# Router table by products, early expert weights, step sizes inside a branch, halves in a scan product, and merge joined with the last projection

## The reference

```python
# first block
h = rmsnorm(x, norm_mix_g) * (1 + sc1) + sh1
y = conformer_conv(h, ...)     # h @ w_in, gated; 31-tap causal conv per channel + b_dw;
                               # silu(layernorm(y)); @ w_out
x = x + g1 * y
h = rmsnorm(x, norm_ffn_g) * (1 + sc2) + sh2
x = x + g2 * hier_moe(h, ...)  # 4 groups x 8 experts, top 2 of the best group, hidden 512
x = rmsnorm(x, final_g)
# second block
h = rms_norm(x) * (1 + scale) + shift
q, k, v, z_att, q_idx, k_idx, w_idx, z_ssm, xbc, dt_raw, gate_logits = split(h @ w_in)
o_att = sparse_attention(...) * silu(z_att)    # an indexer keeps 256 keys for each query
y_att = o_att @ w_branch_att
dt = softplus(dt_raw + dt_bias);  a = -exp(a_log)
y = ssd(xs, dt, a, bm, cm)     # state-space scan, 32 heads of 64, chunks of 128 tokens
y_ssm = rms_norm((y + d_skip * xs) * silu(z_ssm)) @ w_branch_ssm
merged = sigmoid(g_att) * y_att + sigmoid(g_ssm) * y_ssm
x = x + gate * (merged @ w_out)
```

## Time and profile before

| | |
|---|---|
| median of 3 runs | 3097.91 us (3094.88 to 3101.71) |
| profiled execution | 3103.54 us, span 3101.7 us |
| granted TensorE clock, mean | 0.92 |
| TensorE busy | 2635.5 us, 85% of the span |
| VectorE | 1666.2 us, 54% |
| ScalarE | 898.8 us, 29% |
| POOL | 560.5 us, 18% |
| transfers | 430.96 MB, mean 139 GB/s |

### The profile page before, as it was taken

The page is one execution under the profiler, slowest core; times in us unless marked ns, Lnnn a source line. Parts: engine busy times, 40 slices in busy tenths (PEclk is TensorE's granted clock), DMA queues, the critical chain, the costliest instruction groups (busy, mean ns, idle before and its releaser), DMA issues. The chain is left out here.

```text
span 3101.7 us, 39507 instructions
## 1 busy us (share of the span) xinstructions
PE 2635.5 (85%) x15399; PEld 1471.3 (47%) x15399; DVE 1666.2 (54%) x2973; ACT 898.8 (29%) x1333; POOL 560.5 (18%) x504
## 2 busy tenths in 40 slices
PE   5996795598799995887999599969899899899869
PEld 3554344354455552443344377435545545545434
DVE  5884774122222325784999865234734744744651
ACT  5110402121112223333532255123423423423320
POOL 1111032200000002443421000002303303303202
PEclk8998796799999997898899799989999999999989
DMA  8562758399999995110022001320010010010051
GB/s 219 190 203 93 277 190 309 97 375 379 376 381 365 376 328 217 63 47 28 28 75 95 21 1 46 111 75 35 1 61 35 1 61 35 1 62 27 1 217 55
DMA packets 184152, 430.96 MB, mean 139 GB/s; under 512 B 27004, under 2 KB 35452, under 8 KB 183868
## 3 DMA queue, kind: packets, MB, share of 16 engines
q1 hardware_dynamic: 156972, 362.80, 32.7%
q0 software_dynamic: 11088, 33.84, 3.5%
q10 hardware_dynamic: 15936, 32.13, 3.0%
HBM read 370.82 MB, written 57.91 MB: 138 GB/s over the span
## 5 line engine op out<-in xcount | busy, mean ns | idle before, releaser
L1192 PE MATMUL m_gu<-arena,m_xT 128*64 128x256 f32 x1024 | 233.2, 387 | 20.4 <-DMA arena<-in_moe_w_up 18.0
L1194 PE MATMUL m_gu<-arena,m_xT 128*64 128x256 f32 x1024 | 233.2, 387 | 0.0
L2456 POOL TENSOR_TENSOR y_A<-adt,consts 128x1024 f32<-128x1024 f32 x32 | 64.5, 2014 | 882.1 <-POOLq L2240 731.1
L1270 DVE TENSOR_TENSOR m_hid<-m_sg,m_gu 64x256 f32<-64x256 f32 x96 | 39.6, 413 | 337.9 <-ACT m_sg L1240 337.9
L1194 PEld LDWEIGHTS m_gu<-arena,m_xT 128*64 128x64 f32 x1024 | 142.9, 140 | 73.8 <-issue 15.4
L1214 PE MATMUL m_y_ps<-arena,m_hidT 128*64 128x512 f32 x768 | 175.4, 598 | 0.0
L1925 DVE TENSOR_SCALAR_CACHE_REDUCE arena<-arena,s_cand 128x384 bf16<-128x384 f32 (+5 forms) x186 | 166.1, 943 | 2.2
L140 PE MATMUL i_pj<-hT,i_ws 128*128 128x512 f16 x384 | 148.3, 386 | 20.9 <-DVE i_ws L406 12.9
L1192 PEld LDWEIGHTS m_gu<-arena,m_xT 128*64 128x64 f32 x1024 | 142.9, 140 | 38.4 <-issue 27.5
L1240 ACT ACT_TABLE_LOAD x48 | 61.6, 1283 | 322.3 <-issue 274.0
L141 PE MATMUL i_pj<-hT,i_ws 128*128 128x512 f16 x384 | 148.8, 388 | 0.0
(11 more groups left out here) (491 smaller groups left out, 6540.7 us busy)
## 6 DMA issues: line engine op xcount, KB each, us to landing
arena<-in_moe_w_down SPq DMA_DIRECT2D x32, 2048.0 KB, 22.6
arena<-in_moe_w_gate SPq DMA_DIRECT2D x22, 2048.0 KB, 20.4
arena<-in_moe_w_up SPq DMA_DIRECT2D x22, 2048.0 KB, 24.5
hT<-in_moe_w_gate SPq DMA_DIRECT2D x10, 2048.0 KB, 20.1
hT<-in_moe_w_up SPq DMA_DIRECT2D x10, 2048.0 KB, 24.8
conv_y<-in_ada_w SPq DMA_DIRECT2D x8, 2048.0 KB, 7.9
x_tok<-in_ada_w ACTq DMA_DIRECT2D x6, 2048.0 KB, 12.6
slot_out<-m_y ACTq DMA_DIRECT2D x96, 128.0 KB, 6.2
```

Of the source, the lines that this page charges most:

```text
L1192: g = nc.tensor.matmul(gu_ps[i][g_rows, 0:FFN // 2], lhsT=xT[:, c, :], rhs=k.wg[e % WEIGHT_SLOTS][:, c, cols], start=c == 0, stop=c == KC - 1)
L1194: u = nc.tensor.matmul(gu_ps[i][u_rows, 0:FFN // 2], lhsT=xT[:, c, :], rhs=k.wu[e % WEIGHT_SLOTS][:, c, cols], start=c == 0, stop=c == KC - 1)
L2456: nc.gpsimd.tensor_tensor(A[:, s], per_head(k.adt, t, P), k.const("after").unsqueeze(1).to_broadcast([P, HPG, P]), ALU.mult) \
```

## The change

**Convolution and its norm.** The PSUM of the means (`k.mean_ps`) exists from the convolution on and doubles as an accumulator of the first tiles. The mean products of channel tiles 0 to 5 stand ahead of the last tile's taps and those of tile 6 behind them; the norm is left with tile 7's two. The last tile's y is evacuated in two halves and carried by SP and ScalarE (`last_half`) and not by POOL.

```diff
+            pe.wait_ge(u_done, last)
+            means(range(last - 1))
+            taps(last)
+            means(range(last - 1, last))
...
+            last_half(sp, 0)
+            sp.wait_ge(last_in[0], 16 * CG // 2)
...
+            last_half(act, 1)
+            act.wait_ge(last_in[1], 16 * CG // 2)
```

```diff
         def _(sp):
+            load_up(k, sp, 0)
+            load_down(k, sp, 0)
             for t in range(TT):
                 sp.wait_ge(normed_ready, t + 1)
-                sp.dma_start(normed_dram[t * P:(t + 1) * P, :], normed[:, t, :]).then_inc(stored, 16)
+                sp.dma_start(normed_dram[t * P:(t + 1) * P, :], normed[:, t, :]).then_inc(k.normed_stored, 16)
+            load_up(k, sp, 1)
+            load_down(k, sp, 1)
+            load_down(k, sp, 2)
             sp.dma_start(k.x_tok[:, :, :], natural).then_inc(k.x_natural, 16)
-            sp.wait_ge(stored, 16 * TT)
```

```diff
+            nc.tensor.matmul(pos_ps[:, :, :], lhsT=before16[:, :], rhs=mask[:, :, :], start=True, stop=False)
             for t in range(TT):
...
+                last = nc.tensor.matmul(pos_ps[:, t + 1:, :], lhsT=ones16[:, :],
+                                        rhs=mask[:, t:t + 1, :].to_broadcast([P, TT - t, EXPERTS]),
+                                        start=False, stop=t == TT - 1)
...
+            pe.wait_ge(hot, 1)
+            for n in range(2):
+                for t in range(TT):
+                    last = nc.tensor.matmul(tab_ps[:, :], lhsT=low_hot[:, n, t, :], rhs=blk_hot[:, n, t, :],
+                                            start=n == t == 0, stop=n == 1 and t == TT - 1)
...
+            step(v.tensor_tensor(low_hot[:, :, :, :].rearrange(flat), of_all(low, BLOCK), numbers(BLOCK), ALU.is_equal))
+            for n in range(2):
+                step(v.tensor_tensor(low_hot[:, n], low_hot[:, n], bc(tokid[:, :], BLOCK), ALU.mult))
+            v.tensor_tensor(blk_hot[:, :, :, :].rearrange(flat), of_all(blk, TABLE_ROWS), numbers(TABLE_ROWS),
+                            ALU.is_equal).then_inc(hot, 1)
```

```diff
                 last.then_inc(done, 1)
+                if j == 3:
+                    pe.wait_ge(adt_ready, 1)
+                    for n, tri in enumerate(("upto", "after", "ones")):
+                        last = nc.tensor.matmul(sums[n][:, :, :].rearrange("p t h -> p (t h)"), lhsT=k.const(tri),
+                                                rhs=k.adt.rearrange("p t h -> p (t h)"), start=True, stop=True)
+                    last.then_inc(summed, 1)
...
             for j in range(KC):
                 if j + 1 < KC:
                     split(j + 1)
+                if j == 0:
+                    step_sizes()
```

```diff
                     for h in range(HPG):
-                        last = nc.tensor.matmul(yd_ps[:, h * SSM_HD:(h + 1) * SSM_HD], lhsT=M[:, s, h, :],
-                                                rhs=xdt[:, s, h, :], start=True, stop=True)
-                    last.then_inc(q["yd_done"], 1)
+                        for l in (slice(0, P // 2), slice(P // 2, P)):
+                            last = nc.tensor.matmul(yd_ps[l, h * SSM_HD:(h + 1) * SSM_HD], lhsT=M[:, s, h, l],
+                                                    rhs=xdt[:, s, h, :], start=True, stop=True)
+                            if h == HPG - 1:
+                                last.then_inc(q["yd_done"], 1)
```

```diff
+            for c in range(KC):
+                act.wait_ge(w_in[c], 16)
+                high_part(nc, ws[:, 0, c, :], w[:, c % 4, :]).then_inc(high, 1)
+                act.wait_ge(summed, c + 1)
+                nc.scalar.copy(merged[:, 0, c, :], att[:, c % 4]).then_inc(m_high, 1)
...
+            for c in range(KC):
+                dve.wait_ge(sig_in[c % 4], 16 * (c // 4 + 1))
+                nc.vector.tensor_tensor(sig[:, c % 4], sig[:, c % 4], k.y_ssm[:, c, :], ALU.mult).then_inc(mul, 1)
+                dve.wait_ge(mul, c + 1)
+                dve.wait_ge(att_in[c % 4], 16 * (c // 4 + 1))
+                nc.vector.tensor_tensor(att[:, c % 4], att[:, c % 4], sig[:, c % 4], ALU.add).then_inc(summed, 1)
+                if c + 1 < KC:
+                    split(c + 1)
...
+                pool.wait_ge(m_high, c + 1)
+                nc.gpsimd.tensor_tensor(merged[:, 1, c, :], att[:, c % 4], merged[:, 0, c, :], ALU.subtract) \
+                    .then_inc(m_low, 1)
```

534 lines of the change are left out of this document (268 added, 266 removed).

## The result

| | before | changed |
|---|---|---|
| median | 3099.81 us (3094.88 to 3101.82, 4 runs) | 2989.98 us (2986.61 to 2990.49, 4 runs) |
| ratio | | 0.9642 (0.9623 to 0.9661) |
| profiled execution | 3103.54 us, span 3101.7 | 2986.61 us, span 2984.8 |

The account below looks back on a forecast made before the run. The kernel was taken as a row of stages with barriers between, its time their sum. Terms -19 -36 -19.5 -28 -17 +1 = -118.5 us gave 2985 for a like execution, 2979 as median; own range 2968 to 2990, wider 2956 to 3006.

Parts of the forecast that it names:

- rival A2: Scan: each switch between whole and halved array holds TensorE for a pass, so -6 instead of -17: 2990 us; chance 0.05.
- Convolution -7.5 and norm -11.7: Convolution's end and norm: SP and ScalarE carry the last tile, most means come earlier; sum -19 us, bounds -14 to -21.
- Router -36: Router: fp16 counts and a slot table by products instead of scatters; table at 531.9 instead of 567.9 us, weights not limiting.
- Experts 0: Experts keep their length; a gather behind the last 2 MB costs 0 to 5 us, taken as 0; over 618 us means wrong.
- Select +1: Select: two gate tiles, 20.7 us, just hidden in TensorE's idle time at the end; POOL's low parts cost +1 (0 to +4).
- Step sizes -19.5: Step sizes moved into the attention's branch: 23.5 us become 3.9, with 0.8 us of margin for the cover.
- Scan -17: Scan's product in paired halves: -0.8 us a step in 24 of 32 steps; -17 us taken, bounds -26 and +3.
- Merge -28: Merge with last projection: 140.6 us become 112.2, paced by a ScalarE-VectorE ring of 6.5 us a tile; bounds -24, -34.
- A: Scan: the halves of the product bring nothing, 2996 us; chance 0.10.
- E: Scan: every alternation between the halves waits for the pass before, +218 us, 3214 us in all; chance 0.02.
- D: Experts end when their 213 MB have passed whatever their start, so the router's 36 us return: 3015 us; chance 0.03.
- B: Time given back at merge ring (+7), select's store (+3), branch (+2) and gather (+5): 2996 us; chance 0.12.

Follow-up runs that it names:

- the first two runs: Changed kernel with the scan's product of M and xdt whole again, 3001.3 us; changed kernel with all lower half products before all upper ones, 3003.3 us.

## Why the prediction was right

The total (-118.5 forecast, -116.9 between profiled executions) is no balance of large errors: the largest miss of a term is 4.1 us. That the sum comes within 1.6 us is luck all the same: 8.2 us more than forecast (experts, inputs stages, step sizes) stand against 6.5 less (convolution and its norm, "co", router, tokens, select). And the median alone, 2990, would not have told the forecast from rival A2, which put it at just that; the stages tell them apart, and the run with the whole product. By the prediction's own steps:

- **Stages behind barriers, so that their savings add.** Right. Undone alone, the edits give 9.8 + 12.4 - 1.4 (convolution and norm), 17.9 and 23.1 (router), 13.6 (scan, inputs stages included) and 28.4 (merge). The one place where two do not add is the router's zeros. The move of the step sizes was not undone.
- **Convolution -7.5 and norm -11.7.** Right, measured -8.0 and -12.7. The mechanism named, POOL's end behind its queue, is shown by the run that restores it, and its DRAIN of 5.95 us is the time in which the prediction saw nothing to do. The twelve means took 10.4 us as worked out (28 passes, 12.5 us with tile 6's two).
- **Router -36.** Right, -37.2: counts read 1.96 us after the mask's start where 19.56 passed, table 6.3 us after the destinations where 24.2 passed. That the weights would not stand in the way was right. A slip: the counts were not 72 products but 44, which the trace shows as 88 passes; the forecast used the measured 18.40 us and is not touched by it.
- **Experts 0, "a gather behind the last 2 MB costs 0 to 5 us; I take 0".** This term was mis-sized: it cost 2.2 us at the first gather, and the stage was 4.1 us longer. The third expert's up landed 9.8 us into the stage. I had the transfers end at 534 of the old span, when the first gather goes out; they ended some 8 us behind it. The rest of the 4.1 is not settled, since the unedited stage varies by more. The prediction's sign of being wrong, experts longer than 618 us, was badly set: 618 was the length of a window (568.00 to 1186.00) that ends 9.5 us ahead of the stage, and the stage took 627.1 us before the change already.
- **Select +1.** Right in size; but the margin is 11.65 us of idle TensorE and not the 0.3 us taken. The granted clock of the stage was 0.90 in the trace of before and 0.95 in that after, and the stretch in which TensorE works moved with it.
- **Step sizes -19.5.** -18.3. TensorE has no pause over 0.3 us in the branch, so the cover of 0.8 us held; its end is 2.4 us later in the stage, 1.3 for the three products and 1.1 that lie in the stage's first 30 us and that I can't place.
- **Scan -17.** Right as a sum, wrong as a product. The pairs are there, but a step gains 0.56 us and not 0.8, and it does so in all steps but the two in which VectorE is the bound (0.1 to 0.2 us). Of the missing 0.24, 0.10 lies ahead of the first pass (0.31 us from the product before it and not 0.21), 0.05 behind the first pair (0.106 to the second, then 0.052 to 0.058), and 0.05 at the way out (0.16 from the last pair to the next product, where whole passes need 0.11). Another 0.05 was never there to be won: the first of the whole passes is followed after 0.056 us and not 0.112. The first three fit the two switches of the array's form that the changed step adds, and the run with the halves in turn, which has the same switches, shows the same 0.31 ahead; no run has the switches alone. That is rival A2's mechanism, at about 0.1 us a switch and not 0.27. The Trainium skill's rule (TensorEngine Tiling (Array Packing), Key Properties) that a change of tiling mode drains TensorE agrees with this trace, with 0.10 us beside it. What made up for it was the clock: in the first and third scan the segment products of the second step run at the higher level (2.05 us instead of 3.44), and these two scans are 1.0 us shorter than the other two (131.4 and 131.5 against 132.4). The inputs stages gave 2.7 back.
- **Merge -28.** Right, -28.2, with two errors that cancel: the ring is 6.75 and not 6.5, TensorE begins at 11.6 and not at 13.2. The 6.8 us that followed from the exclusive lock was the better value. By the Trainium skill (SBUF — State Buffer, Who interferes with whom, "The single rule") VectorE and POOL can't both use the shared ports; the runs agree, with 2.29 us for an operation of 1.22 that meets the last 1.2 us of POOL's.

Of the rivals, A and E are refuted by the first two runs, D by the experts' length (631.2, where D needed 663): their first reload came 44.6 us into the stage, 42.7 before, so the whole supply moved along; B's price came about at one of its four places (the gather), C's at none.

## What to carry to other kernels

In a row of stages behind barriers, count for each who ends the last idle time, and price every edit in its own stage; undone one at a time, such edits add up to within a few microseconds. Where two engines exclude each other at a port, moving a small operation from the slow one to the fast one helps both, even if the fast one is the busier: 2.12 us of POOL's became 1.22 of VectorE's. And a large transfer that nobody waits for yet sets the time as soon as a small one that somebody does wait for is asked for behind it: the zeros of a table behind gate 0 and 1 in one queue, the first gather beside the third expert's weights in two.

## What was not expected of the hardware

- POOL's queue takes 8.4 us from its last issue to the end of the stage, in two kernels alike (8.44 and 8.43), when the data had landed after 2.0; 5.95 us of it are its DRAIN. Ended by ScalarE's queue, the stage needs 2.4 us for the same kind of transfers, with DRAINs of 0.01 us on SP and ScalarE.
- VectorE and POOL shut each other out both ways: whichever has begun goes on to its end, and the other's operation is recorded as lasting through the wait (POOL's 3.10 us for 2.12, VectorE's 3.03 or 2.29 for 1.22).
- Single passes of 64-column weights come every 0.058 us on one half of the array, the same pitch as pairs on both: 1.90 us for 32 singles, 1.15 for 16 pairs.
- The clock at a stage's start was not the same for the same work: the same inputs stage was granted 0.57 or 0.79 in its first 8 us, with the same instructions in it and in the 30 us before it. What decides it, no run here shows.
